# Filler products, another order of the sums of squares, a later division of x, and one 512-column product per FFN in a fourteen-stage transformer kernel

## The chip, the cores and the metric

The kernel runs on one core of one Trainium2 chip. The metric is the time of one execution in microseconds (us), as the median of a few runs. The profile was taken of one further execution.

## What is computed

Two transformer blocks follow each other on x of 256 tokens by 1024 features, in float32. The first has two layers of FFN, mixer, cross attention to a memory, FFN, with one norm ahead of each part; the mixers are a banded plus stick-breaking attention ("even") and a dilated attention ("odd"). The second has two layers of FFN, mixer ("mix": differential attention and a chunked linear recurrence, gated and merged), FFN, where the output of every part is normed once more before it is added:

```python
for l in range(DEPTH):                      # second block, cut
    h = rmsnorm(x, ffn1_norm_pre[l])
    x = x + 0.5 * rmsnorm(swiglu(h, ffn1_w_gu[l], ffn1_w_down[l]), ffn1_norm_post[l])
    h = rmsnorm(x, mix_norm_pre[l])
    ...                                     # attention, recurrence, gates -> merged
    x = x + rmsnorm(merged @ w_out[l], mix_norm_post[l])
    h = rmsnorm(x, ffn2_norm_pre[l])
    x = x + 0.5 * rmsnorm(swiglu(h, ffn2_w_gu[l], ffn2_w_down[l]), ffn2_norm_post[l])
```

## The kernel before

**Data.** x lies transposed in SBUF: 8 chunks c of 128 features by 256 tokens. Every weight matrix comes as one stream of 829 tiles of 128 by 1024 float32 (512 KB). SyncE loads tile n into one of 4 buffers `raw` once `lo_split` says that tile n-4 has been split. ScalarE rounds it to `w_hi` (L1053), VectorE makes the rest, `w_lo` = raw - w_hi (L1487); both have 6 slots. The activations are held as such a pair too (`a_hi`, `a_lo`, side by side in one tensor). A tile is multiplied chunk by chunk with three matmuls of 256 columns: w_hi by hi, w_hi by lo, w_lo by hi, so 24 matmuls to a tile, all recorded under L461 (`mm`).

**Stages.** ffn0, even, xa0, ffn1, ffn2, odd, xa1, ffn3, ffn4, mix0, ffn5, ffn6, mix1, ffn7. An FFN has 66 tiles: gate and up for each of 22 blocks j, and a down tile two blocks later. Tiles 0, 1 and 2 (gate 0, up 0, gate 1) are multiplied side by side, chunk by chunk, as the chunks of the normed x arrive (`first_three`); tile 3 (up 1) follows, then gate 2, up 2, down 0, gate 3, up 3 (tile 8), down 1, and then a loop. All engines have their own instruction list in a fixed order with semaphores between them.

**A norm.** ScalarE squares the 8 chunks into `sq` (L1084), they are added up over chunks, and a float32 product with a matrix of ones on TensorE adds over partitions; each such product shows as two records. ScalarE takes the root (L1068), VectorE the reciprocal (L1506), by which the first outputs are multiplied (L1634 and so on). After ffn4 to ffn7 the output has a norm of its own: VectorE adds the squares of chunks 0 to 5 (`part_of_squares`, L1547), and `sum_of_parts` multiplies that sum and then the squares of chunks 6 and 7. After a mix stage `sum_chunk` multiplies the squares of every chunk by itself, one behind each output tile.

**x times the root.** To avoid a reciprocal there, `post_norm` (L1598, L1602) keeps x multiplied by the root `rt`. Later x has to be divided by it: `inverse_scale` (L1553) takes the reciprocal into `rstd_m`, and `restore_x` (L1558) multiplies the 8 chunks. In an FFN both run on VectorE between the low parts of block 1 and the loop; in a mix stage `restore_x` runs between the last output tile's split and `post_norm`.

The line numbers below are those of the profile.

Of the kernel before, what the change touches and what calls it, by code (L numbers as in the profile page):

```python
# [29 lines left out]
P = 128  # L30
D = 1024
T = 256
C = D // P
# [5 lines left out]
RAW = 4  # L39
RING = 6  # L40
# [101 lines left out]
def build(nc, stream_d, x_d, mem_d, vec_d, con_d, biasa_d, biasc_d, heads_d, out_d, stages=STAGES):  # L142
    total = sum(TILES[s] for s, _ in stages)
    with ExitStack() as ctx:
# [50 lines left out]
        STAT = 6  # L195
# [5 lines left out]
        def gate_up_of(j, after_mixer):  # L201

            return bank[4 + 2 * (j % 2)][:, 0:T], bank[2 if j == 0 and after_mixer else 5 + 2 * (j % 2)][:, 0:T]
# [240 lines left out]
        def _(pe):  # L444
# [10 lines left out]
            att = [None]  # L455
            act_of = {"a": (a_hi, a_lo), "b": (b_hi, b_lo)}
            fresh = {}
            rescaled = [False]

            def mm(out, lhsT, rhs, start, stop, shared=False):  # L460
                return nc.tensor.matmul(out, lhsT, rhs, start=start, stop=stop, skip_group_check=shared)  # L461
# [81 lines left out]
            def sum_squares(stat=STAT):  # L543
# [17 lines left out]
                t.next(sq_made, C)  # L561

            def sum_of_parts():

                base = t.so_far(sq_made)
                t.next(sq_made, C)
                pe.wait_ge(root_ready, t.next(root_ready) - 1)
                pe.wait_ge(sq_second, t.next(sq_second))
                mm(bank[STAT][:, 0:T], ones, sq[:, 0, :], True, False)
                for c in (C - 2, C - 1):  # L570
                    pe.wait_ge(sq_made, base + c + 1)
                    last = mm(bank[STAT][:, 0:T], ones, sq[:, c, :], False, c == C - 1)
                last.then_inc(ss_ready, 1)

# [25 lines left out]
            def ffn(k, after_mixer):  # L600
# [4 lines left out]
                def first_three():  # L605
# [4 lines left out]
                    for c in range(C):  # L610
                        ready(c)
                        for i in range(3):
# [5 lines left out]
                            if c == C - 1:  # L618
                                last.then_inc(tile_mm, 1)

                def gate_up(n, slot, j, J):
                    for part, freed in ((0, gate_read), (1, up_read)):
                        pe.wait_ge(freed, J - 1)
                        w_tile(n + part, (slot + part) % RING, gate_up_of(j, False)[part], hi, lo)

# [14 lines left out]

                (hi, lo), h = act_of["a"], act_of["b"]
                s0 = n0 % RING
# [17 lines left out]
                at[0] += FFN_TILES  # L660
                if k >= 4:
                    sum_of_parts()
                t.next(x_ready, C)

# [303 lines left out]
            def mixer(kind, layer):  # L968
# [14 lines left out]
                if kind == "xa":  # L983
                    act_of["a"], act_of["b"] = act_of["b"], act_of["a"]
                if kind == "even":
                    stick()
# [23 lines left out]
                for k in range(C):  # L1010
                    w_next("b", y_ready)
                    if k:
                        sum_chunk(k - 1)
                sum_chunk(C - 1)
                t.next(x_ready, C)

            previous = "ffn"
            for stage, index in stages:
# [451 lines left out]
        def _(dve):  # L1470
# [143 lines left out]
            def ffn(k, following, after_mixer):  # L1614
# [58 lines left out]
                h_low(1, base + 1)  # L1673
                if rescaled[0]:
                    inverse_scale()
                    restore_x()
                first = n0 + 4 + AHEAD
                rounds = (FJ - 2) // 4
                if n0 + FFN_TILES == total:
                    rounds -= 1  # L1680
                with dve.Fori(0, rounds) as i:
                    for u in range(4):
                        def splits(e, u=u):
                            m = first + 3 * u + e
                            split(i * 12 + m, m % RAW, m % RING)
                        step(u % 2, i * 12 + (n0 + 4 + 3 * u), i * 4 + (base + 2 + u), splits)
                done[0] = first + 12 * rounds
# [311 lines left out]
            def mixer(kind, layer, following):  # L1999
# [59 lines left out]
                for k in range(C):  # L2059
                    next_tile()  # L2060
                    turn[0] += 1
                restore_x()
                dve.wait_ge(y_ready, t.next(y_ready, C))
# [290 lines left out]
```

## Time and profile before

| | us |
|---|---|
| median of 3 runs | 2635.38 (2631.01 to 2637.68) |
| the profiled execution, its own time | 2623.86 |
| its span, first to last instruction | 2622.1 |
| TensorE matmuls busy | 2545.0 (97%) |
| VectorE busy | 1802.4 (69%) |
| ScalarE busy | 1396.5 (53%) |
| mean granted TensorE clock | 0.991 |

The stages lie on the span like this, by the kernel's order and the trace: ffn4 ends at about 1400, mix0 runs to 1716, ffn5 to 1911.5, ffn6 to 2102, mix1 to 2419, ffn7 to the end. "Busy" of TensorE counts a stretch in which matmuls follow each other without a gap as full, whatever their distance from start to start; the number of matmuls in a stretch tells the distance. The profiled execution was 11.5 us shorter than the median of the runs.

### The profile page before, as it was taken

The numbers are of one execution on the slowest core, as the hardware profiler recorded it, in microseconds if no ns is written. First come the engines' busy times: TensorE is split into PE (matmuls) and PEld (weight loads), VectorE is DVE, ScalarE is ACT, GpSimd is POOL, SyncE is SP. The second block draws the span as 40 slices with busy tenths as digits, with TensorE's granted clock in tenths as the row PEclk, the third lists the DMA queues.
The fourth block names the chain that finished last, engine by engine and source line by source line (L and its number), as shares of the span: only waits on it lengthen the run. The fifth ranks groups of instructions, "written<-read, shape, count | busy, mean of one in ns | idle before, by whom it ended". The sixth has DMA issues, their size and how long they took to land.

```text
span 2622.1 us, 56431 instructions
## 1 busy us (share of the span) xinstructions
PE 2545.0 (97%) x21370; PEld 2468.5 (94%) x21370; DVE 1802.4 (69%) x2868; ACT 1396.5 (53%) x2232; POOL 190.6 (7%) x265
## 2 busy tenths in 40 slices
PE   8999799999999999999999999999999989999998
PEld 8998699999998899999998998989989989989998
DVE  6667686667667585767667657786686676676865
ACT  5456556445445655545445555654454465555543
POOL 0001001000000201000000250000000005300000
PEclk9999899999999999999999999999999999999999
DMA  7664244765564344655654543545545545335553
GB/s 270 208 192 137 81 145 157 234 211 188 195 194 155 105 164 142 201 193 180 203 193 147 182 146 113 169 161 185 184 161 192 193 147 174 129 115 176 175 193 113
DMA packets 122826, 445.89 MB, mean 170 GB/s; under 512 B 13688, under 2 KB 14712, under 8 KB 122688
## 3 DMA queue, kind: packets, MB, share of 16 engines
q1 hardware_dynamic: 120816, 436.79, 50.8%
q0 software_dynamic: 1872, 7.17, 0.8%
q8 instruction: 98, 1.61, 0.3%
q14 instruction: 40, 0.33, 0.0%
HBM read 442.86 MB, written 1.05 MB: 169 GB/s over the span
## 4 chain that ended last, share of the span: by engine, by line
PE 92%; DVE 5%; ACT 2%; issue 1%; DMA 0%; SPq 0%; DVEq 0%; ACTq 0%
PE bank L461 91%; DVE w_lo L1487 1%; PE bank L823 1%; DVE x L1558 1%; ACT w_hi L1053 1%; DVE z L1598 0%; DVE rstd_x L1506 0%; DVE x L1602 0%; DVE rstd_m L1553 0%; DVE score L1547 0%; DVE a L1514 0%; DMA raw<-in_stream_dram 0%; ACT score L1285 0%; DVE score L1538 0%; DVE z L1902 0%
## 5 line engine op out<-in xcount | busy, mean ns | idle before, releaser
L461 PE MATMUL bank<-a,w_hi 128*128 128x256 f32 x7472 | 1311.2, 280 | 37.6 <-DVE a L1514 28.0
L461 PEld LDWEIGHTS bank<-a,w_hi 128*128 128x128 f32 x7472 | 1137.1, 189 | 52.1 <-issue 47.4
L1487 DVE TENSOR_TENSOR w_lo<-raw,w_hi 128x1024 fp32r<-128x1024 f32 x829 | 1012.6, 1225 | 212.4 <-ACT w_hi L1053 210.8
L461 PE MATMUL bank<-a,w_lo 128*128 128x256 f32 x3736 | 1039.0, 278 | 0.0
L1053 ACT CAST w_hi<-raw 128x1024 fp32r<-128x1024 f32 x829 | 842.3, 1045 | 57.3 <-DMA raw<-in_stream_dram 53.8
L461 PE MATMUL bank<-b,w_hi 128*128 128x256 f32 x4800 | 839.3, 278 | 1.0 <-DVE b L1487 1.0
L461 PEld LDWEIGHTS bank<-b,w_hi 128*128 128x128 f32 x4800 | 726.8, 188 | 8.5 <-issue 3.6
L461 PEld LDWEIGHTS bank<-a,w_lo 128*128 128x128 f32 x3736 | 707.7, 189 | 0.0
L461 PE MATMUL bank<-b,w_lo 128*128 128x256 f32 x2400 | 664.9, 277 | 0.0
L461 PEld LDWEIGHTS bank<-b,w_lo 128*128 128x128 f32 x2400 | 451.4, 188 | 0.0
L1113 ACT CAST b<-hmid 128x256 fp32r<-128x256 f32 x132 | 53.8, 407 | 401.0 <-PE bank L461 389.7
L1625 DVE TENSOR_TENSOR hmid<-bank,rstd_x 128x256 f32<-128x256 f32 x168 | 71.2, 424 | 163.6 <-PE bank L461 163.5
L1109 ACT ACTIVATE sil<-sil 128x256 f32<-128x256 f32 x176 | 73.6, 418 | 145.7 <-DVE sil L1620 145.7
L1487 DVE TENSOR_TENSOR b<-hmid,b 128x256 fp32r<-128x256 f32 x132 | 56.0, 425 | 128.3 <-ACT b L1113 128.3
L461 PE MATMUL bank<-w_hi,a 128*128 128x256 f32 x736 | 130.7, 281 | 0.0
L2163 POOL TENSOR_SCALAR score<-score,rr 128x128 f32<-128x128 f32 (+1 forms) x96 | 44.5, 479 | 1114.7 <-DVE rr L1842 817.5
L461 PEld LDWEIGHTS bank<-w_hi,a 128*128 128x128 f32 x736 | 111.9, 188 | 3.4 <-issue 2.5
L1716 DVE TENSOR_TENSOR z<-bank,rstd_x 128x256 f32<-128x256 f32 x125 | 52.8, 422 | 79.0 <-PE bank L461 78.4
L461 PE MATMUL bank<-w_lo,a 128*128 128x256 f32 x368 | 102.2, 278 | 0.0
L1113 ACT CAST a<-hmid 128x256 fp32r<-128x256 f32 x44 | 17.9, 407 | 136.1 <-PE bank L461 132.5
L1639 DVE TENSOR_TENSOR hmid<-sil,hmid 128x256 f32<-128x256 f32 x176 | 74.8, 425 | 5.7
L1620 DVE TENSOR_TENSOR sil<-bank,rstd_x 128x256 f32<-128x256 f32 x160 | 67.8, 424 | 12.7 <-PE bank L461 2.8
(193 smaller groups left out, 1897.1 us busy)
## 6 DMA issues: line engine op xcount, KB each, us to landing
raw<-in_stream_dram SPq DMA_DIRECT2D x829, 512.0 KB, 3.7
z<-in_biasc_dram POOLq DMA_DIRECT2D x6, 512.0 KB, 4.9
z<-in_biasa_dram POOLq DMA_DIRECT2D x3, 512.0 KB, 4.7
x<-in_x_dram SPq DMA_DIRECT2D x2, 512.0 KB, 8.0
v<-in_mem_dram POOLq DMA_DIRECT2D x2, 512.0 KB, 5.9
out_dram<-x SPq DMA_DIRECT2D x8, 128.0 KB, 1.8
con<-in_con_dram POOLq DMA_DIRECT2D x1, 912.0 KB, 6.6
vec<-in_vec_dram POOLq DMA_DIRECT2D x1, 417.0 KB, 5.6
```

Source lines behind the costliest of these rows:

```text
L461: return nc.tensor.matmul(out, lhsT, rhs, start=start, stop=stop, skip_group_check=shared)
L823: last = nc.tensor.transpose(out[:, col:col + P], p[:, src:src + P], ident)
L1053: nc.scalar.copy(w_hi[:, slot, :], raw[:, raw_slot, :]).then_inc(hi_split, 1)
L1109: nc.scalar.activation(sil[:, jj, :], sil[:, jj, :], ACT.Silu).then_inc(silu_done, 1)
L1113: nc.scalar.copy(high_of["b"][:, jj, :], hmid[:, jj, :]).then_inc(hhi_done, 1)
L1487: return nc.vector.tensor_tensor(out, a, hi.bitcast(F32), ALU.subtract)
L1558: ins = nc.vector.tensor_tensor(x[:, c, :], x[:, c, :], rstd["m"][:, :], ALU.mult)
L1620: nc.vector.tensor_tensor(sil[:, j % 2, :], gate_up_of(j, after_mixer)[0], r, ALU.mult)\
L1625: nc.vector.tensor_tensor(hmid[:, j % 2, :], gate_up_of(j, after_mixer)[1], r, ALU.mult)\
L1639: nc.vector.tensor_tensor(hmid[:, jj, :], sil[:, jj, :], hmid[:, jj, :], ALU.mult)\
L1716: nc.vector.tensor_tensor(z[:, tile, :], out[:, 0:T], rstd[norm][:, :], ALU.mult).then_inc(w_evac, 1)
L2163: last = nc.gpsimd.tensor_scalar(p, p, rr[:, k, b:b + 1], 1.0, ALU.mult, ALU.mult)
```

## The change

- `keep_going(n)` issues n float32 products of the ones matrix with 256 columns of constants into a bank that nobody reads at that time: 1 ahead of and 7 behind `sum_of_parts` (none behind the last), 1 ahead of and 6 behind the last `sum_chunk` of a mix stage. At the kernel's start 20 products of 256 columns run on the first rounded weight tile as soon as it is there.
- `sum_of_parts` multiplies chunks 6 and 7 first and VectorE's sum last.
- In an FFN the VectorE loop is cut in two, 2 rounds and the rest, and `inverse_scale` and `restore_x` run between the two. A round is 12 tiles. In a mix stage `restore_x` runs behind the second of the last eight tiles.
- In every FFN one product of 512 columns (both halves of chunk 0, with the weights of tile 4) runs between tile 3 and tile 4, into bank 0, which the first down tile overwrites.

```diff
+            def keep_going(n):
+                for _ in range(n):
+                    mm(bank[T_BANK][:, 0:T], ones, con[:, 0:T], True, True)
 def sum_of_parts():
...
-                pe.wait_ge(sq_second, t.next(sq_second))
-                mm(bank[STAT][:, 0:T], ones, sq[:, 0, :], True, False)
                 for c in (C - 2, C - 1):
                     pe.wait_ge(sq_made, base + c + 1)
-                    last = mm(bank[STAT][:, 0:T], ones, sq[:, c, :], False, c == C - 1)
-                last.then_inc(ss_ready, 1)
+                    mm(bank[STAT][:, 0:T], ones, sq[:, c, :], c == C - 2, False)
+                pe.wait_ge(sq_second, t.next(sq_second))
+                mm(bank[STAT][:, 0:T], ones, sq[:, 0, :], False, True).then_inc(ss_ready, 1)
...
+                def wide_product(slot):
+                    mm(bank[0][:, :], w_hi[:, slot, 0:P], both[:, 0, :, :].rearrange("p a t -> p (a t)"), True, True)
...
                     for part, freed in ((0, gate_read), (1, up_read)):
                         pe.wait_ge(freed, J - 1)
+                        if j == 2 and part == 0:
+                            wait_split(n)
+                            wide_product(slot)
...
                 if k >= 4:
+                    keep_going(1)
                     sum_of_parts()
+                    keep_going(7 if k < 7 else 0)
...
+                keep_going(1)
                 sum_chunk(C - 1)
+                keep_going(6)
...
+            pe.wait_ge(hi_split, 1)
+            for _ in range(20):
+                mm(bank[T_BANK][:, 0:T], w_hi[:, 0, 0:P], w_hi[:, 0, 0:T], True, True)
...
-                if rescaled[0]:
-                    inverse_scale()
-                    restore_x()
...
-                with dve.Fori(0, rounds) as i:
...
+                for done_rounds, more in ((0, 2), (2, rounds - 2)):
+                    if done_rounds and rescaled[0]:
+                        inverse_scale()
+                        restore_x()
+                    with dve.Fori(0, more) as i:
...
                 for k in range(C):
                     next_tile()
                     turn[0] += 1
-                restore_x()
+                    if k == 1:
+                        restore_x()
```

## Rows read from the trace of the kernel before

**Rows 1.** The page: busy time by engine, and the chain's shares.

```profile
PE 2545.0 (97%) x21370; PEld 2468.5 (94%) x21370; DVE 1802.4 (69%) x2868; ACT 1396.5 (53%) x2232; POOL 190.6 (7%) x265
...
PE 92%; DVE 5%; ACT 2%; issue 1%; DMA 0%; SPq 0%; DVEq 0%; ACTq 0%
```

**Rows 2.** Windows: PE, PEld, DVE, ACT, POOL busy (x count), clock, DMA share, GB/s.

```profile
11.13:14.48 3.35, 3.35 (x16) 3.35 (x17) 2.62 (x7) 3.35 (x11) 2.24 (x4) 1.00 1.03 421
...
1404.00:1407.00 3.00, 0.46 (x4) 0.49 (x5) 2.96 (x8) 2.05 (x5) 0.00 (x0) 1.00 0.00 0
1407.10:1410.50 3.40, 3.40 (x19) 3.40 (x18) 3.40 (x11) 2.45 (x6) 0.00 (x0) 0.50 0.00 0
...
1721.10:1724.50 3.40, 3.24 (x15) 3.27 (x16) 3.40 (x11) 2.46 (x7) 0.00 (x0) 0.51 0.00 0
...
2127.30:2130.70 3.40, 3.40 (x19) 3.40 (x18) 3.40 (x5) 0.61 (x1) 0.00 (x0) 0.50 0.67 219
```

**Rows 3.** Timeline of the end of ffn4: start us, duration us, instruction [idle before it].

```profile
1399.97 1.80 DVE L1547 TENSOR_TENSOR score<-score 128x256 f32<-128x256 f32 x4
...
1401.92 1.53 PE L461 MATMUL bank<-score,con 128*128 128x256 f32 x6 [1.41 <-DVE score L1547]
1403.49 0.47 ACT L1068 ACTIVATE rt<-bank,eps 128x256 f32<-128x256 f32 x1 [2.29 <-PE bank L461]
```

**Rows 4.** Timeline of the end of mix0.

```profile
1708.41 1.23 DVE L1487 TENSOR_TENSOR w_lo<-raw,w_hi 128x1024 fp32r<-128x1024 f32 x1 [1.95 <-ACT w_hi L1053]
...
1715.91 2.77 DVE L1558 TENSOR_TENSOR x<-x,rstd_m 128x256 f32<-128x256 f32 x8
...
1716.76 0.30 PEld L461 LDWEIGHTS bank<-score,con 128*128 128x128 f32 x2 [0.44 <-ACT score L1084]
1717.49 0.48 ACT L1068 ACTIVATE rt<-bank,eps 128x256 f32<-128x256 f32 x1 [0.53 <-PE bank L461]
...
1718.71 0.42 DVE L1598 TENSOR_TENSOR z<-x,rt 128x256 f32<-128x256 f32 x1
```

**Rows 5.** Timeline of the beginning of ffn5.

```profile
1733.56 1.75 DVE L1506 RECIPROCAL rstd_x<-rstd_x 128x256 f32<-128x256 f32 x1 [0.43 <-ACT rstd_x L1068]
...
1737.39 0.47 PE L461 MATMUL bank<-a,w_hi 128*128 128x256 f32 x2 [0.27 <-DVE w_lo L1487]
...
1741.44 1.75 DVE L1553 RECIPROCAL rstd_m<-rt 128x256 f32<-128x256 f32 x1
...
1747.60 0.47 PE L461 MATMUL bank<-a,w_hi 128*128 128x256 f32 x2 [1.49 <-DVE w_lo L1487]
```

**Rows 6.** Timeline of the beginning of ffn6.

```profile
1930.02 1.75 DVE L1506 RECIPROCAL rstd_x<-rstd_x 128x256 f32<-128x256 f32 x1 [0.57 <-ACT rstd_x L1068]
...
1944.06 0.47 PE L461 MATMUL bank<-a,w_hi 128*128 128x256 f32 x2 [1.80 <-DVE w_lo L1487]
```

**Rows 7.** Timeline inside ffn5's loop: one step of VectorE and ScalarE.

```profile
1770.97 2.00 ACT L1053 CAST w_hi<-raw 128x1024 fp32r<-128x1024 f32 x2
1772.05 1.23 DVE L1487 TENSOR_TENSOR w_lo<-raw,w_hi 128x1024 fp32r<-128x1024 f32 x1 [0.70 <-ACT w_hi L1053]
```

**Rows 8.** Windows: matmuls in long even stretches of ffn1 (two), ffn5 and ffn6.

```profile
420.00:440.00 20.00, 20.00 (x172) 20.00 (x171) 17.28 (x29) 15.52 (x27) 3.08 (x3) 1.00 0.69 211
460.00:600.00 140.00, 140.00 (x1238) 140.00 (x1237) 90.61 (x122) 64.99 (x89) 2.65 (x5) 1.00 0.66 218
...
1750.00:1900.00 150.00, 150.00 (x1276) 150.00 (x1275) 95.34 (x129) 68.84 (x93) 0.00 (x0) 1.00 0.60 197
...
1950.00:2090.00 140.00, 140.00 (x1237) 140.00 (x1237) 90.88 (x125) 65.36 (x89) 0.00 (x0) 1.00 0.62 203
```

**Rows 9.** Timeline of the kernel's start.

```profile
4.17 1.04 ACT L1053 CAST w_hi<-raw 128x1024 fp32r<-128x1024 f32 x1 [2.14 <-DMA raw<-in_stream_dram]
...
11.13 0.77 PE L461 MATMUL bank<-a,w_hi 128*128 128x256 f32 x2 [11.13 <-DVE a L1514]
...
22.02 0.48 ACT L1068 ACTIVATE rstd_x<-bank,eps 128x256 f32<-128x256 f32 x1 [2.81 <-PE bank L461]
```

More of the change, by code:

```diff
@@ L456, in _ @@
             act_of = {"a": (a_hi, a_lo), "b": (b_hi, b_lo)}
+            two_of = {"a": a_two, "b": b_two}
             fresh = {}
@@ L639, in down @@
                     last.then_inc(tile_mm, 1)
-                (hi, lo), h = act_of["a"], act_of["b"]
+                (hi, lo), h, both = act_of["a"], act_of["b"], two_of["a"]
                 s0 = n0 % RING
@@ L984, in mixer @@
                     act_of["a"], act_of["b"] = act_of["b"], act_of["a"]
+                    two_of["a"], two_of["b"] = two_of["b"], two_of["a"]
                 if kind == "even":
@@ L1680, in ffn, with splits @@
                     rounds -= 1
-                with dve.Fori(0, rounds) as i:
[L1682 to L1686, printed above, removed]
+                for done_rounds, more in ((0, 2), (2, rounds - 2)):
[3 more added lines that the diff above has]
+                    with dve.Fori(0, more) as i:
+                        for u in range(4):
+                            def splits(e, u=u):
+                                m = first + 12 * done_rounds + 3 * u + e
+                                split(i * 12 + m, m % RAW, m % RING)
+                            step(u % 2, i * 12 + (n0 + 4 + 12 * done_rounds + 3 * u),
+                                 i * 4 + (base + 2 + 4 * done_rounds + u), splits)
                 done[0] = first + 12 * rounds
```

## Prediction

> **What bounds the kernel now.** I read the page first: TensorE's matmuls fill 97% of the span and 92% of the chain that ended last [rows 1]. So nothing that VectorE, ScalarE or the DMA do matters except where TensorE waits for it, and the questions are where TensorE stands still, where its clock is low, and how far apart its matmuls start while it is "busy". The chain in order of time showed where other engines enter it: stick-breaking in the even mixer, which the change does not touch, and the seams ffn4-mix0, mix0-ffn5, ffn5-ffn6, ffn6-mix1, mix1-ffn7 and the end.
>
> At the seams I read windows and the timeline. Behind ffn4 TensorE waits 1.41 us for VectorE's sum, runs the three sum products in 1.53 us [rows 3] and then waits about 3 us for root, product and low part of chunk 0: 0.46 us busy in the next 3 [rows 2]. Behind this gap the granted clock is 0.50 for 3.4 us: 19 matmuls in 3.40 us at 1.2 GHz against some 30 at 2.4 [rows 2]. The same stands at mix0-ffn5 [rows 2], ffn5-ffn6 and mix1-ffn7. In mix1 the low stretch comes 20 us later, behind other waits [rows 2].
>
> In the heads of ffn5, 6 and 7 TensorE later waits twice for `w_lo`: 0.27 us at tile 5, and 1.49, 1.80 and 1.49 us at tile 8, because VectorE takes the reciprocal and divides x there (1.75 us, then 8 multiplications in 2.8 us) [rows 5, 6].
>
> Last, the spacing. At full clock, 1238 matmuls fill 140 us of ffn1: 113.1 ns from start to start. The same instructions in ffn5 need 150 us for 1276: 117.6 ns [rows 8]. ffn1 itself runs 172 in 20 us (116 ns) before its sum product and 113 ns after it. So there are two paces at one clock, about 4.5 ns apart; a pace, once taken, stays until TensorE waits or runs a float32 product, and it is taken anew at each restart. In this trace ffn5 kept the slow one from tile 8 to its end: 58 tiles x 24 x 4.5 ns = 6.3 us.
>
> **The change, part by part.**
>
> *Order of the sums (ffn4 to ffn7).* Three products take 1.53 us, 0.45 from start to start and 0.17 of modelled end [rows 3]. Two of them leave the path behind VectorE's sum: 0.9 us each time. In front of them now stand a filler (0.45) and the two others, whose last square ends some 0.4 us before VectorE's sum; that queue delays the last product by 0 to 0.25. I take 0.8 x 4 = 3.2 us. In the mix heads everything that follows hangs on VectorE's chain (products, fold of the squares, low parts, two reciprocals), so there this is the only gain, whatever the clock.
>
> *Last sum of a mix stage.* The root is ready at 1717.97, VectorE starts its products at 1718.71 because the division of x ran until then [rows 4]. Moved behind the second output tile the division is free: VectorE idles about 1.95 us per tile there [rows 4]. That is 0.74 saved. The filler ahead of the last sum product has only 0.44 us of gap [rows 4] behind the product before it and lasts 0.45, with its weight loads: I charge 0.3. Net 0.44 x 2 = 0.9 us.
>
> *Fillers behind the sums.* 7 x 0.45 = 3.2 us stand between the last sum product and the first low part about 3.1 us later; 6 x 0.45 = 2.7 in a gap of 3.6. Free, if the first products of the norm are not ready sooner. They do no work; their worth is the clock. If it stays at 2.4 GHz, the 19 matmuls of 3.40 us take about 2.15 (19 x 0.113). The 1.25 to 1.5 us are not all path: chunks arrive every 1.13 us and need 9 x 0.113 = 1.02, so TensorE then follows VectorE. What shows is the wait that disappears: the reciprocal's idle of 0.43, 0.57 and 0.43 us for the root, which waits for TensorE's sum in tile 3 [rows 5, 6]. 1.4 us together; lower bound 0, if the clock falls all the same; upper 1.5 x 3, if VectorE's order did not bind.
>
> *Later division in the FFN.* The waits at tile 8 go: 1.49 + 1.80 + 1.49, and 0.17 each by which the last matmul's modelled end hides idle time: 5.3 us. The work (4.5 us) goes into the loop. There VectorE finishes the low half of a tile at 1773.28, and that tile is four behind the one that TensorE has just begun at 1770.5 [rows 7]: used at about 1781.7, 8 us later. 4.5 fit in, and VectorE idles over 2 us per step, so the lead is back after two steps. If it did not fit, TensorE would stop once per FFN, up to the whole 4.5. Next late is tile 5, whose wait grows to about 1 us since TensorE arrives earlier; this is in the sum, since all is counted from VectorE's chain. Cutting the loop in two adds a loop end, under the same cover.
>
> *Wide product.* No row shows 512 columns; two of 256 take 0.227 us [rows 8], which I take as price; 0 where a wait follows. In ffn5 to 7 tile 5's wait swallows it, in ffn0 to 4 nothing does: 5 x 0.22 = 1.1 us lost. Bank 0 is free then.
>
> *Start.* The first rounded tile is there at 5.2 us, the first real product at 11.13 [rows 9], and 16 matmuls run in 3.35 us until 14.48 before the pace doubles [rows 2]: at most 1.5 us to win. 20 products at the low clock (0.213 each) fill 5.3 to 9.6. Whether the clock is up at 11.13, after 1.5 us or more of idling, is open: between 0 and 1.5, and VectorE's three copies allow only 0.9 of it up to the reciprocal. I take 0.8. On this the Trainium skill (TensorE: Matmul & The Clock Gate, Part 1) says that the monitor's window runs freely and does not begin with the kernel, so that the number of slow matmuls differs from run to run; by it this term is anything from 0 to 1.5 in any one run. The trace cannot contradict it with one start.
>
> *mix1's low stretch* at 2127 [rows 2] may stay, vanish or get a twin in mix0, since TensorE idles there a little more: 0, plus or minus 1.7.
>
> **The sum:** 3.2 + 0.9 + 1.4 + 5.3 + 0.8 - 1.1 = 10.5 us. From 2623.86 of the profiled execution: 2613.4. The runs shown have a median 11.5 us higher, at 2635.38; I take the gain as the same there and predict 2624.9.
>
> **Rivals.**
>
> *Pace for the better.* The 11.5 us between median and profiled execution are close to two further FFNs at the slow pace (2 x 6.3): the timed runs may well have ffn5, 6 and 7 all slow. If fewer restarts and the wide product leave one or two more FFNs at the fast pace, 6 to 13 us come on top: 2612 to 2619. For: float32 products between others did end the slow pace in ffn1 [rows 8]. Against: tile 5's wait comes behind the wide product, and the pace is taken anew after it; the restart at tile 8 led to the slow pace in ffn5 and to the fast one in ffn6 [rows 8]. The Trainium skill (same page, Part 2 on issue gaps and LDWEIGHTS) has loads pulled ahead of running matmuls and prices 128 weight columns at 107 ns, 256 moving columns at 109; by that one long product gives the loads a lead, and this rival would hold. Its 109 ns agree with neither pace here (113.1 and 117.6); the measurements decide.
>
> *No use of fillers or order (same).* The clock falls in spite of fillers, the start wins nothing, and the queue eats the reordering: 5.3 + 1.5 + 1 of the sums - 1.1 = 6.7 us or less: 2629. For: the clock also fell at 2127, where no long gap of TensorE lies ahead [rows 2]. Against: with the fillers TensorE is busy nearly throughout.
>
> *Pace for the worse (slower).* If the wide product turned the pace slow in ffn0 to ffn4, where it is fast now and no wait follows that would change it, each would lose 62 x 24 x 4.5 ns = 6.7 us, five 33: 2658. From two FFNs on it outweighs the whole gain. For: nobody has seen what it does; a pace is sticky. Against: the float32 products, as long, led to the fast one.
>
> **Numbers.** The sum as it stands 0.5 (2618 to 2630, since terms and one pace may go either way), pace for the better 0.22, no use 0.18, pace for the worse 0.1. A measurement can tell 0.3%, 7.9 us: faster means below 2627.5. Of the first case four fifths lie there, of the second all, of the third a fifth; faster 0.66, same 0.24, slower 0.10. The range 2611 to 2634 holds the first three but for their edges.
>
> **What the profile after would show.** Clock 1.00 at all five seams; three sum products with VectorE's last; PE's waits for `w_lo` in ffn5 to 7 once, about 1 us at tile 5, none at tile 8; L1553 and L1558 in the loop's middle with no wait of PE near them; matmul counts per 140 us of every FFN. The prediction is wrong if those counts change (1238 or 1190), if PE waits in the middle of an FFN, or if the fillers still run when the first low part is ready.

## The result and the profile after

The changed kernel takes 2654.26 us (median of 8 runs, 2645.55 to 2661.74), the kernel before 2634.34 us beside it (8 runs, 2626.21 to 2642.14): a ratio of 1.0082, 95% interval 1.0060 to 1.0104. It is 0.8% slower. The forecast was 2624.9 with a range of 2611 to 2634, so the result lies on the other side and far outside. The profiled execution took 2658.42 us (span 2656.6), 34.6 us more than the profiled execution of before.

The page of after, busy time by engine and the chain's shares:

```profile
PE 2608.1 (98%) x21476; PEld 2529.5 (95%) x21476; DVE 1803.0 (68%) x2868; ACT 1396.9 (53%) x2232; POOL 190.5 (7%) x265
...
PE 93%; DVE 4%; ACT 2%; issue 0%; DMA 0%; SPq 0%; DVEq 0%; ACTq 0%
```

Against [rows 1], TensorE is busy for 63.1 us more with 106 more records; VectorE has 0.6 us more. The 106 records are the 39 float32 products of two records each, the 20 at the start and the 8 wide ones; at 0.43, 0.213 and 0.23 us a product that is some 23 us. For the other 40 the same matmuls take longer, or stand further apart. Windows inside the FFNs of after (columns as in [rows 2]) show it:

```profile
460.00:600.00 140.00, 140.00 (x1191) 140.00 (x1190) 89.62 (x122) 63.02 (x86) 2.64 (x5) 1.00 0.65 215
650.00:790.00 140.00, 140.00 (x1191) 140.00 (x1190) 87.75 (x120) 62.79 (x86) 0.00 (x0) 1.00 0.60 196
...
1265.00:1405.00 140.00, 140.00 (x1191) 140.00 (x1190) 88.33 (x121) 62.86 (x86) 0.00 (x0) 1.00 0.60 195
1780.00:1920.00 140.00, 140.00 (x1238) 140.00 (x1237) 95.10 (x133) 65.64 (x89) 0.00 (x0) 1.00 0.61 201
1970.00:2110.00 140.00, 140.00 (x1191) 140.00 (x1190) 90.72 (x126) 61.90 (x86) 0.00 (x0) 1.00 0.59 192
```

The clock reads 1.00 in all of them, and 1191 matmuls are through where [rows 8] had 1238 in ffn1. All five of ffn0 to ffn4 read 1191, ffn6 and ffn7 too; ffn5, the slow one of before, is now the fast one. Where does ffn0 change? The timeline of TensorE around its wide product:

```profile
24.18 0.28 PE L462 MATMUL bank<-a,w_lo 128*128 128x256 f32 x1
24.29 0.39 PE L462 MATMUL bank<-a,w_hi 128*128 128x256 f32 x2
24.52 0.28 PE L462 MATMUL bank<-a,w_lo 128*128 128x256 f32 x1
24.63 0.62 PE L462 MATMUL bank<-a,w_hi 128*128 128x512 f32 x3
25.09 0.28 PE L462 MATMUL bank<-a,w_lo 128*128 128x256 f32 x1
...
25.44 0.28 PE L462 MATMUL bank<-a,w_lo 128*128 128x256 f32 x1
...
25.80 0.28 PE L462 MATMUL bank<-a,w_lo 128*128 128x256 f32 x1
```

A group of three matmuls (one of `w_lo`, two of `w_hi`) starts 0.34 us after the one ahead of it before the product, and 0.35 to 0.36 us after it behind the product (the timeline rounds to 0.01). From one `w_lo` to the next across the product it is 0.57 us: 0.23 more than a group, so the product itself costs what two of 256 columns would, as forecast. What follows it is what costs.

The end of ffn4 and the beginning of ffn5 in after, timelines:

```profile
1434.95 0.60 PE L462 MATMUL bank<-con 128*128 128x256 f32 x2
1435.68 1.53 PE L462 MATMUL bank<-score,con 128*128 128x256 f32 x6
1437.05 3.19 PE L462 MATMUL bank<-con 128*128 128x256 f32 x14
1437.25 0.47 ACT L1088 ACTIVATE rt<-bank,eps 128x256 f32<-128x256 f32 x1 [1.44 <-PE bank L462]
...
1752.93 0.47 ACT L1088 ACTIVATE rt<-bank,eps 128x256 f32<-128x256 f32 x1 [0.65 <-PE bank L462]
1753.51 0.42 DVE L1618 TENSOR_TENSOR z<-x,rt 128x256 f32<-128x256 f32 x1 [2.20 <-ACT rt L1088]
1756.06 0.47 PE L462 MATMUL bank<-a,w_hi 128*128 128x256 f32 x2 [0.58 <-DVE a L1534]
...
1767.84 1.75 DVE L1526 RECIPROCAL rstd_x<-rstd_x 128x256 f32<-128x256 f32 x1
...
1771.66 0.47 PE L462 MATMUL bank<-a,w_hi 128*128 128x256 f32 x2 [0.38 <-DVE w_lo L1507]
...
1835.29 1.75 DVE L1573 RECIPROCAL rstd_m<-rt 128x256 f32<-128x256 f32 x1
1837.07 2.77 DVE L1578 TENSOR_TENSOR x<-x,rstd_m 128x256 f32<-128x256 f32 x8
1840.07 1.23 DVE L1507 TENSOR_TENSOR w_lo<-raw,w_hi 128x1024 fp32r<-128x1024 f32 x1 [0.23 <-DVE x L1578]
```

ScalarE idles 1.44 us ahead of its root behind ffn4, where [rows 3] had 2.29: 0.85 won. VectorE starts its products 0.58 us after the root's start at the end of mix0, where [rows 4] had 1.22: 0.64 won. The reciprocal of ffn5's head has no idle time before it any more ([rows 5]: 0.43). The only wait for `w_lo` in this head is 0.38 us, at tile 5. The division runs at 1835, in mid-FFN, with no wait of TensorE beside it. So the named gains are there, and over them lies a loss of another kind.

### The profile page after: what moved, and what is told of

Its sections match the earlier page's. It is cut to its first block, busy times and chain, and to the rows that moved or that the text cites. A ratio compares the mean times of both kernels' runs of the same rounds, so it can differ in the third digit from the quotient of the medians.

```text
span 2656.6 us, 56661 instructions
## 1 busy us (share of the span) xinstructions
PE 2608.1 (98%) x21476; PEld 2529.5 (95%) x21476; DVE 1803.0 (68%) x2868; ACT 1396.9 (53%) x2232; POOL 190.5 (7%) x265
## 4 chain that ended last, share of the span: by engine, by line
PE 93%; DVE 4%; ACT 2%; issue 0%; DMA 0%; SPq 0%; DVEq 0%; ACTq 0%
PE bank L462 92%; PE bank L837 1%; DVE x L1622 1%; DVE z L1618 1%; DVE w_lo L1507 0%; DVE a L1534 0%; DVE score L1558 0%; DVE rstd_x L1526 0%; DMA x<-in_x_dram 0%; ACT score L1305 0%; ACT w_hi L1073 0%; ACT a L1094 0%; DVE z L1924 0%; DVE z L1927 0%; DVE z L1930 0%
## 5 line engine op out<-in xcount | busy, mean ns | idle before, releaser
L462 PE MATMUL bank<-a,w_hi 128*128 128x256 f32 x7478 | 1333.0, 282 | 9.0 <-DVE w_lo L1507 6.4
L462 PE MATMUL bank<-b,w_hi 128*128 128x256 f32 x4802 | 857.2, 281 | 1.0 <-DVE b L1507 1.0
L462 PEld LDWEIGHTS bank<-b,w_hi 128*128 128x128 f32 x4802 | 737.3, 189 | 8.4 <-issue 3.6
```

## The experiments

All compare with the kernel before, run on the same chip beside them. Where a kernel adds products, their outputs are overwritten or read by nothing, and no part of the computation is left out; kernels that take fillers away leave out only such products. In the diffs `wide_product(slot, n)` multiplies `n` columns of both activation blocks into bank 0, and `float_product(out)` multiplies the constant ones with 256 float32 columns (0.45 us).

The kernel before has medians of 2627.31 to 2631.46 us in these comparisons and 2634.34 in the first, so two kernels that were not compared side by side are best compared by their ratios.

Since several kernels are compared by place, here is the difference to the profiled execution of before in each stage, in us. It is taken at the moment when VectorE ends the low part of the same stream tile, up to the end of the span.

| stage | after | e1, no wide | e5, float32 at tile 7 | e7, e5 without fillers |
|---|---|---|---|---|
| start to tile 6 | +0.1 | -1.3 | -1.1 | +1.4 |
| rest of ffn0, mixer | +7.3 | -1.7 | 0.0 | -2.2 |
| ffn1 to ffn4, mixer between | +26.0 | +0.3 | -1.1 | +0.7 |
| end of ffn4 | +0.4 (+0.9 of pace, -0.4 behind it) | -0.9 | -0.9 | -0.9 |
| mix0 | +1.6 | +5.0 | +3.3 | 0.0 |
| head of ffn5 | -3.7 | -2.8 | -3.1 | -2.3 |
| rest of ffn5 | -5.1 | 0.0 | -5.1 | -5.1 |
| head of ffn6 | -2.4 | -3.4 | -3.1 | -1.4 |
| rest of ffn6, mix1 | +7.6 | -0.9 | +0.8 | -1.7 |
| head of ffn7 | -2.2 | -3.1 | -2.4 | -2.2 |
| rest | +5.1 | -0.6 | -0.6 | -0.6 |
| sum | +34.6 | -9.1 | -13.3 | -14.2 |

**e1_after_no_wide**: the changed kernel without its wide product.

```diff
-                        if j == 2 and part == 0:
-                            wait_split(n)
-                            wide_product(slot)
```

> The changed kernel without its 512-column product, all else kept. Theory (the 512-column product turns TensorE's pace from 113 to 117.6 ns per matmul, and nothing turns it back until the FFN ends): ffn0 to ffn4 are back at about 1238 matmuls per 140 us, 5 x 6.7 = 33 us shorter than the changed kernel, so about 2620 us, and 10 us under the kernel before; ffn5 to 7 may lie at either pace. Rival (the fillers at the start and the seams, or the cut loop of VectorE, set the slow pace): ffn0 to ffn4 stay at 1191 per 140 us and the time at about 2654.

Measured: 2614.29 us (6 runs, 2604.97 to 2618.22) beside 2627.31, ratio 0.9947 (0.9929 to 0.9966). One of its windows, in ffn4:

```profile
1250.00:1390.00 140.00, 140.00 (x1238) 140.00 (x1237) 88.57 (x120) 62.85 (x86) 0.00 (x0) 1.00 0.60 194
```

ffn0 to ffn4 are fast again; ffn5 is slow, ffn6 and ffn7 fast, as in before. Eight products of 0.23 us, 1.8 us of work, are worth some 35 us by the ratios (1.0082 against 0.9947) and 40 by the medians.

**e2_only_wide**: the kernel before with only the wide product, at the same place.

```diff
+                        if j == 2 and part == 0:
+                            wait_split(n)
+                            wide_product(slot)
```

> The kernel before with nothing but the 512-column product between tiles 3 and 4 of each FFN. Theory: ffn0 to ffn4 at 1191 per 140 us, 33 us and 1 us of products over the kernel before, about 2668 us. Rival (the product only does harm together with fillers or the cut loop): at most 2 us over the kernel before, 1238 per 140 us.

Measured: 2672.69 us (4 runs, 2651.90 to 2676.18), ratio 1.0149 (1.0103 to 1.0195). All eight FFNs are at the slow pace in its profile, of 2676.18 us:

```profile
460.00:600.00 140.00, 140.00 (x1191) 140.00 (x1190) 88.04 (x120) 62.96 (x86) 2.65 (x5) 1.00 0.65 215
```

By these two the wide product alone sets the loss, with or without the other edits.

**e3_mixed**: before, with a different insert in each of ffn0 to ffn4 ahead of tile 4, and a float32 product in ffn5 to ffn7 at tile 8, behind its wait.

```diff
+                        if j == 2 and part == 0:
+                            wait_split(n)
+                            if k == 0:
+                                wide_product(slot, 256)
+                            if k in (1, 2, 4):
+                                wide_product(slot)
+                            if k == 1:
+                                wide_product(slot)
+                            if k == 2:
+                                float_product(bank[0][:, 0:T])
+                        if k >= 5 and j == 3 and part == 1:
+                            wait_split(n + 1)
+                            float_product(gate_up_of(j, False)[part])
```

> The kernel before with another insert in each FFN in place of the 512-column product, so that one trace shows which of them turns the pace. ffn0: one float32r product of 256 columns; ffn1: two of 512; ffn2: one of 512 and behind it a float32 product of 256; ffn3: nothing; ffn4: one of 512; ffn5 to 7: nothing before tile 4, but a float32 product of 256 columns at tile 8, behind its wait for w_lo. If length against the weight load matters: ffn0 and ffn3 1238 per 140 us, ffn1 and ffn4 1191, ffn2 1238 since the float32 product sets the fast pace, and ffn5 to 7 all 1238. If a 512-column product toggles the pace: ffn1 is fast. If float32 products do not set the pace (rival: coincidence in the trace before), ffn2 stays slow and ffn5 to 7 are mixed.

Measured: 2643.47 us (one execution). Its windows in ffn1 (two wide products) and ffn4 (one):

```profile
460.00:600.00 140.00, 140.00 (x1238) 140.00 (x1237) 90.01 (x123) 64.87 (x88) 2.63 (x5) 1.00 0.66 219
...
1250.00:1390.00 140.00, 140.00 (x1191) 140.00 (x1191) 85.61 (x116) 61.03 (x83) 0.00 (x0) 1.00 0.57 190
```

ffn0 (one of 256 columns), ffn1 (two wide), ffn2 (wide, then float32) and ffn3 (nothing) are fast, ffn4 (one wide) is slow. In ffn1 the second wide product takes back what the first did. Behind tile 8's wait a float32 product set nothing: ffn5 and ffn6 came out slow, ffn7 fast.

**e4_float_behind_wait**: after without the wide product, with one float32 product in a running stream in ffn5 and ffn7 and behind tile 5's wait in ffn6.

```diff
+                        if k in (5, 7) and j == 3 and part == 0:
+                            wait_split(n)
+                            float_product(gate_up_of(j, False)[part])
+                        if k == 6 and j == 2 and part == 1:
+                            wait_split(n + 1)
+                            float_product(gate_up_of(j, False)[part])
```

> The changed kernel without its 512-column product, with one float32 product of ones by constants (256 columns, 0.45 us) in ffn5 and ffn7 ahead of tile 7 and in ffn6 at tile 5 behind its wait. Theory: all eight FFNs at the fast pace, 1238 per 140 us; about 6.7 us less for each of ffn5 to 7 that is slow in the run without it, so 2610 to 2614 us, and a smaller spread from run to run. Rival (the pace behind a restart is not to be set): mixed paces in ffn5 to 7 and the time of the run without the product.

Measured: 2612.36 us (4 runs, 2611.14 to 2614.62), ratio 0.9947 (0.9927 to 0.9967). ffn5 and ffn7 are fast and ffn6 is slow (1191 in 140 us). Only ffn5 speaks for the product in the stream: 5.4 us ahead of it hold 47 matmuls there, but 49 in ffn7, as many as behind it, so ffn7 was fast already. In ffn6 the stream was slow ahead of the wait, and the product behind the wait left it so.

**e5_float_tile7**: after without the wide product, and a float32 product ahead of tile 7 in ffn5, ffn6 and ffn7, behind their last wait.

```diff
+                        if k >= 5 and j == 3 and part == 0:
+                            wait_split(n)
+                            float_product(gate_up_of(j, False)[part])
```

> The changed kernel without the 512-column product and with one float32 product ahead of tile 7 in ffn5, ffn6 and ffn7, where TensorE does not wait. Theory (a float32 product amid running matmuls sets the fast pace, one behind a wait does not): all eight FFNs at 1238 per 140 us, 6 us under the run that had the product of ffn6 behind a wait, about 2606 us. Rival (ffn5 and ffn7 were fast by chance in that run): one or two of the three are slow, 2612 to 2618 us.

Measured: 2610.68 us (6 runs, 2607.37 to 2613.32) beside 2630.29, ratio 0.9916 (0.9892 to 0.9941): the lowest median of all, though the intervals of e1, e4, e6 and e7 overlap with it. Windows ahead of the product in ffn5, behind it, and over ffn5:

```profile
1736.70:1742.20 5.50, 5.50 (x48) 5.50 (x48) 5.49 (x10) 4.08 (x6) 0.00 (x0) 1.00 0.67 203
...
1743.00:1748.50 5.50, 5.50 (x50) 5.50 (x50) 4.54 (x8) 3.40 (x6) 0.00 (x0) 1.00 0.91 316
...
1755.00:1895.00 140.00, 140.00 (x1238) 140.00 (x1237) 92.53 (x129) 63.53 (x86) 0.00 (x0) 1.00 0.57 194
```

48 against 50 in equal stretches (each count includes the matmuls cut by the edges): slow, then fast. The same in ffn6 and ffn7. So all eight are fast, and e5 is 5.1 us better than e1 just in "rest of ffn5".

**e6_no_start** and **e7_no_fillers**: e5 without the 20 products at the start; and without any filler.

```diff
-            for _ in range(20):
-                mm(bank[T_BANK][:, 0:T], w_hi[:, 0, 0:P], w_hi[:, 0, 0:T], True, True)
...
-                    keep_going(1)
                     sum_of_parts()
-                    keep_going(7 if k < 7 else 0)
...
-                keep_going(1)
                 sum_chunk(C - 1)
-                keep_going(6)
```

> The same without the 20 products at the start. Theory (they raise the clock for the first products in some runs only): 0 to 1.3 us slower in the median; in the profile the first 3.4 us behind the first real product at half clock. Rival (they change the pace of ffn0): ffn0 at 1191 per 140 us.

> The same without any filler product, at the start or at the seams. Theory (the seam fillers hold the clock at ffn5, ffn6 and ffn7, which shows as the wait of the reciprocal for the root, 1.4 us in all, while the order of sums and the division keep their gains): 1.4 to 3 us slower than with all fillers, the clock 0.50 behind each seam again. Rival (the fillers carry most of the gain): 6 us or more slower.

Measured: e6 2612.41 us (5 runs, 2609.29 to 2612.97), ratio 0.9917 (0.9889 to 0.9945); e7 2611.43 us (7 runs, 2609.61 to 2618.41), ratio 0.9933 (0.9911 to 0.9955). All three intervals overlap; no filler is worth anything that can be measured here. Where the clock was low, first in e5, then in e7:

```profile
1423.40:1426.80 3.40, 3.40 (x18) 3.40 (x18) 3.25 (x7) 1.05 (x1) 0.00 (x0) 0.51 0.80 276
...
2116.30:2119.70 3.40, 3.40 (x19) 3.40 (x18) 3.40 (x7) 1.05 (x1) 0.00 (x0) 0.51 0.92 294
```

```profile
1405.70:1409.10 3.40, 3.40 (x17) 3.40 (x17) 3.40 (x11) 2.48 (x7) 0.00 (x0) 0.50 0.00 0
...
1423.00:1426.40 3.40, 2.22 (x19) 2.25 (x20) 3.40 (x5) 0.04 (x1) 0.00 (x0) 1.00 0.36 125
```

e5 has its low stretches inside the mix stages, four of them, and none at a seam; e7 has them at the seams and none inside. In the table the fillers win 0.8, 1.7 and 0.2 us in the three heads (e5 against e7) and lose 3.3 in mix0 and 2.5 in "rest of ffn6, mix1". The other traces bear this out, with numbers that change from one to the next: with the seam fillers mix0 holds no low stretch in e10, one in after, e4 and e9, and two in e1, e5, e6 and e11, and costs 0.7, 1.4 to 1.6 and 3.2 to 5.0 us more than in before. In those seven a low stretch begins some 21 to 23 us behind the root of ffn4's end, and in none of the six without fillers. So in mix0 the low stretch was mostly moved, not saved.

**e8_toggles**: before, with other inserts, at tile 4 and, in ffn1 and ffn3, once more ahead of tile 7.

```diff
+                            if k in (0, 1, 3):
+                                wide_product(slot)
+                            if k == 0:
+                                wide_product(slot)
+                                wide_product(slot)
+                            if k == 2:
+                                wide_product(slot, 384)
+                            if k == 4:
+                                wide_product(slot, 128)
+                        if j == 3 and part == 0 and k in (1, 3):
+                            wait_split(n)
+                            if k == 1:
+                                mm(bank[6][:, :], w_hi[:, slot, 0:P], both[:, 0, :, :].rearrange("p a t -> p (a t)"), True, True)
+                            else:
+                                float_product(bank[6][:, 0:T])
```

> The kernel before with another insert ahead of tile 4 in each FFN. ffn0: three products of 512 columns; ffn1: one of 512, and one of 512 ahead of tile 7; ffn2: one of 384; ffn3: one of 512, and a float32 product ahead of tile 7; ffn4: one of 128. Theory (each 512-column product turns the pace over, a float32 product within a stream sets the fast one): ffn0 slow (1191 per 140 us), ffn1 fast from tile 7 on (1238), ffn3 fast from tile 7 on. ffn2 and ffn4 tell which lengths turn it; if an odd number of half products does, both are slow. Rival (one 512-column product sets the slow pace and the fast ffn1 of the mixed run was chance): ffn1 slow.

Measured: 2660.64 us (one execution). Its windows: ffn0; ffn1 between its two wide products and behind them; ffn3; ffn4:

```profile
30.00:170.00 140.00, 140.00 (x1191) 140.00 (x1190) 87.98 (x120) 62.47 (x86) 2.11 (x4) 1.00 0.61 210
455.90:464.30 8.40, 8.40 (x72) 8.36 (x72) 8.40 (x15) 6.56 (x11) 0.00 (x0) 1.00 0.52 172
470.00:610.00 140.00, 140.00 (x1238) 140.00 (x1237) 89.54 (x123) 63.27 (x86) 2.63 (x5) 1.00 0.63 215
...
1080.00:1220.00 140.00, 140.00 (x1191) 140.00 (x1190) 86.10 (x117) 60.42 (x82) 0.00 (x0) 1.00 0.55 187
1270.00:1410.00 140.00, 140.00 (x1191) 140.00 (x1191) 85.60 (x117) 60.60 (x83) 0.00 (x0) 1.00 0.55 186
```

Three wide products leave ffn0 slow, as one does. In ffn1 the first slows the stream and the second, three tiles later, makes it fast. 128 columns act like 512 (ffn4), 384 like 256 (ffn2 fast, 1238). And the float32 product of ffn3, in a running stream, did not cure what a wide product had done: it is no sure remedy. The traces hold many more such cases, since each FFN has sum products of its own. In ffn5 to ffn7 it is one, in the middle of tile 3; with the inserted ones at tile 7, one float32 product in a running stream met a slow pace 28 times in the fourteen traces, and the pace was fast behind it 17 times and slow 11 times. A fast pace it left fast, 27 times of 27. In ffn0 to ffn4 two such products stand in a row ahead of tile 3, and wherever they ran without a wait in front the pace was fast behind them: 53 times from slow, as in ffn1 of before [rows 8], and 12 times from fast. That is how ffn0 to ffn4 come to be fast in before. Two in a row at tile 7, as a remedy, were not tried.

**e9_two_wide**: after, with the wide product twice.

```diff
                             wide_product(slot)
+                            wide_product(slot)
```

> The changed kernel with a second 512-column product right behind the first in every FFN: more work, nothing taken away. Theory (each such product turns the pace over, two leave it as it was): ffn0 to ffn4 at 1238 per 140 us, about 33 us under the changed kernel and 1 to 2 us over it without any such product, about 2616 us. Rival (any 512-column product sets the slow pace, or costs time by itself): 2655 us or more.

Measured: 2619.47 us (10 runs, 2612.61 to 2629.85) beside 2631.46, ratio 0.9958 (0.9932 to 0.9984). ffn0 to ffn4 read 1237 or 1238:

```profile
460.00:600.00 140.00, 140.00 (x1237) 140.00 (x1237) 90.69 (x124) 64.27 (x88) 2.64 (x5) 1.00 0.66 220
```

Eight more products, and the kernel is some 33 us faster than after by the ratios, 35 by the medians. It is the plainest test of the theory: no cost that grows with the products, by their duration, banks or operands, can be the cause, since all are doubled.

ffn5 to ffn7 are fast too, and two of them show what a pure toggle can't explain. In ffn5 the pace was slow ahead of the two products, 0.35 to 0.36 us from one `w_lo` to the next, and fast behind them, 0.34:

```profile
1738.78 0.28 PE L462 MATMUL bank<-a,w_lo 128*128 128x256 f32 x1
...
1739.14 0.28 PE L462 MATMUL bank<-a,w_lo 128*128 128x256 f32 x1
...
1742.03 0.28 PE L462 MATMUL bank<-a,w_lo 128*128 128x256 f32 x1
...
1742.37 0.28 PE L462 MATMUL bank<-a,w_lo 128*128 128x256 f32 x1
```

ffn6 went the same way. So two wide products led to the fast pace from either one; they don't simply leave it as it was.

**e10_old_division**: e5 with the division of x back in the FFN's head.

```diff
+                if rescaled[0]:
+                    inverse_scale()
+                    restore_x()
...
-                    if done_rounds and rescaled[0]:
-                        inverse_scale()
-                        restore_x()
```

> The changed kernel without the 512-column product, with the float32 product ahead of tile 7, and with the division of x in the FFNs back at its old place (in the mix stages it stays at the new one). Theory: waits of 1.5 to 2 us for w_lo at tile 8 of ffn5, 6 and 7 come back, 5 us in all, and with them a new draw of the pace behind tile 8, up to 6.3 us for each FFN that draws the slow one: 2616 to 2630 us and a wide spread. Rival (the later division gains nothing, since VectorE only idles elsewhere): 2611 us.

Measured: 2625.02 us (10 runs, 2613.03 to 2631.28), ratio 0.9981 (0.9953 to 1.0009): 14 us above e5 by the medians, about 17 by the ratios. TensorE waits 11.1 us for `w_lo` in the whole profile, ten times, against 7.2 and seven times in e5: 3.9 us. The rest is the pace. The wait at tile 8 lies behind the float32 product and drew anew; ffn5 and ffn7 came out slow:

```profile
2465.00:2605.00 140.00, 140.00 (x1191) 140.00 (x1190) 86.08 (x116) 60.62 (x82) 0.00 (x0) 1.00 0.54 179
```

ffn0 was slow too in this execution (1192), with nothing changed there. It was slow from its first tiles on, ahead of the sum products: 62 matmuls in the 7 us from 12 on, first here, then in e5, 64:

```profile
12.00:19.00 7.00, 7.00 (x62) 7.00 (x61) 4.58 (x11) 6.89 (x16) 3.79 (x6) 1.00 0.92 365
```

```profile
12.00:19.00 7.00, 7.00 (x64) 7.00 (x64) 4.53 (x9) 6.85 (x15) 3.31 (x6) 1.00 0.88 357
```

**e11_old_order**: e5 with the sum products in their old order, VectorE's first.

```diff
+                pe.wait_ge(sq_second, t.next(sq_second))
+                mm(bank[STAT][:, 0:T], ones, sq[:, 0, :], True, False)
                 for c in (C - 2, C - 1):
                     pe.wait_ge(sq_made, base + c + 1)
-                    mm(bank[STAT][:, 0:T], ones, sq[:, c, :], c == C - 2, False)
-                pe.wait_ge(sq_second, t.next(sq_second))
-                mm(bank[STAT][:, 0:T], ones, sq[:, 0, :], False, True).then_inc(ss_ready, 1)
+                    last = mm(bank[STAT][:, 0:T], ones, sq[:, c, :], False, c == C - 1)
+                last.then_inc(ss_ready, 1)
```

> The same as the last but with the new division, and with the old order of the three sum products at the end of ffn4 to ffn7. Theory: 0.8 us each, 3.2 us slower than with the new order, about 2614 us. Rival (with the filler in front the order is worth nothing): 2611 us.

Measured: 2615.85 us (10 runs, 2609.33 to 2617.56), ratio 0.9943 (0.9919 to 0.9966). Its interval overlaps that of e5, so by the time this is open; the sign and size (about 5 us) don't contradict 3.2. The profiled execution had ffn0 slow as well, so it can't be compared with e5's as a whole. But the term can be read off at its place. ScalarE's wait ahead of the root at ffn4's end, in e11 and then in e5:

```profile
1407.36 0.47 ACT L1093 ACTIVATE rt<-bank,eps 128x256 f32<-128x256 f32 x1 [2.28 <-PE bank L462]
```

```profile
1400.40 0.47 ACT L1092 ACTIVATE rt<-bank,eps 128x256 f32<-128x256 f32 x1 [1.44 <-PE bank L462]
```

At the ends of ffn4 to ffn7 it is 2.28, 2.28, 2.29 and 1.99 us with the old order and 1.44 each time with the new: 3.1 us together, with the filler in front in both.

**e12_before_again**: the kernel before, unchanged, profiled a second time.

> The kernel before, profiled once more. Theory (its runs spread by 20 us because ffn5, 6 and 7 draw their pace anew at tile 8): another set of slow FFNs than ffn5 alone, ffn0 to ffn4 fast again, and the time of the run off 2623.9 by about 6.3 us for each slow FFN more or less. Rival (the spread has another source): the same paces and another time, or the same time and other paces.

Measured: 2630.21 us, 6.35 us more than the first profile. Its windows in ffn5, ffn6 and ffn7:

```profile
1760.00:1900.00 140.00, 140.00 (x1191) 140.00 (x1191) 86.17 (x118) 61.37 (x84) 0.00 (x0) 1.00 0.58 191
1955.00:2095.00 140.00, 140.00 (x1237) 140.00 (x1237) 90.06 (x123) 64.33 (x87) 0.00 (x0) 1.00 0.61 199
2460.00:2600.00 140.00, 140.00 (x1191) 140.00 (x1190) 87.64 (x118) 62.54 (x84) 0.00 (x0) 1.00 0.56 186
```

ffn7 is slow here and was fast in the first profile. Ahead of tile 8's wait the stream of ffn7 is slow in both profiles; behind it, it is fast in the first and slow in the second. Up to the end of mix1 the two profiles are 0.4 us apart, at the last tile of ffn7 5.9 us; 6.3 were computed for one slow FFN. The same program takes one path or the other.

## Why the prediction was wrong

**The step that failed** is the one on the wide product: "two of 256 take 0.227 us, which I take as price", "5 x 0.22 = 1.1 us lost". The price of the product itself was right (0.23 us across it). But the step took the price as the whole effect, although the paragraph on spacing had shown two sticky paces, and left the effect on the pace to a rival, at a chance of 0.1. That rival, "each would lose 62x24x4.5 ns = 6.7 us, five 33: 2658", is what happened. Between their first and last tiles ffn0 to ffn4 lost 6.4 to 7.0 us each, 33 together (the table's rows have 33.3 and 0.9 at the end of ffn4, about 1 of it in the mixers between). e1 and e2 show that the product is the cause; e3, e8 and e9 that its effect is a turn of the pace and no cost in itself. The argument against that rival, "the float32 products, as long, led to the fast one", compared products by their duration, and not even that was alike: a float32 product takes 0.43 to 0.45 us, and only each of its two records, 0.22, is about as long as the wide product's 0.23. In e8 the shortest of all, 128 columns, turns the pace as 512 do, and 384 leave it.

**ffn5 to ffn7.** "In ffn5 to 7 tile 5's wait swallows it" held for the cost and not for the pace. In ffn5 of after the 24 matmuls between the product and tile 5's wait are fast where the stream ahead was slow, in ffn6 and ffn7 they are slow where it was fast, and behind the wait each stayed so to its end (-5.1, +4.7 and +5.1 us). Whether the product or the wait settled these three isn't shown, since a wait can change the pace. "The pace is taken anew after a wait" is supported by e3, e4, e10 and e12, but anew doesn't mean another: of 53 waits of over 0.1 us in the heads of ffn5 to ffn7, over all fourteen traces and without those that have an insert right behind them, 18 turned a fast pace slow, 4 a slow one fast, and 31 left it. Ffn5 of before was slow from tile 5's wait on, not only from tile 8's, as the prediction had it. One consequence of the draws was left out of the forecast: the later division, by removing tile 8's wait, also removes a draw. The 3.9 us of e10's waits and two slow FFNs at some 5 us, as in its profile, are about the 14 us it costs, where the waits alone were priced at 5.3; that its timed runs had two slow FFNs on average isn't shown.

**Order of the sums (3.2).** The root's wait behind ffn4 is 0.85 us shorter, and the stage gave 0.9 in e1, e5 and e7; 0.8 was forecast. In after only 0.4 of it is left when the next stage's first tiles are reached. The roots' waits of e11 against e5 give 3.1 us over the four ends; in time e11 can't tell it from nothing.

**Last sum and division of a mix stage; clock fillers; later division.** The heads of ffn5, ffn6 and ffn7 gained 3.7, 2.4 and 2.2 us in after and 2.8, 3.4 and 3.1 in e1, against about 2.5, 3.3 and 2.5 by the forecast's terms. The waits at tile 8 are gone in all three, as said; tile 5's is 0.4 to 0.5 us in after, where the wide product fills part of it, and 0.5 to 0.8 in e1, not 1. The division in the loop disturbed nothing.

**The fillers' worth (1.4)** is the second step that failed. They did hold the clock at all seams, and the heads gained from it (0.8 + 1.7 + 0.2 us, e5 against e7). But in e5 mix0 and mix1 hold two low stretches each, 3.4 us at half speed, where before had one in mix1 [rows 2] (and one in mix0 as well in e12) and e7 none, and they gave back more. The prediction had this as "plus or minus 1.7", centred on nothing; it should have been charged in both mixes. Since e7 can't be told from e5 in time, the value for the sum is 0 as far as is shown. The windows of after in the two mix heads:

```profile
1458.70:1462.10 3.40, 3.16 (x15) 3.19 (x16) 3.40 (x7) 0.00 (x0) 0.00 (x0) 0.51 0.59 171
...
2155.00:2158.40 3.40, 3.29 (x15) 3.32 (x16) 3.40 (x6) 0.21 (x1) 0.00 (x0) 0.50 0.60 172
```

**The start (0.8).** 0 in after, 1.3 in e1 and 1.1 in e5, but 1.5 lost in e9; e6 and e7, without it, lost 1.0 and 1.4 against before. In after 17 matmuls ran in 3.72 us at the low pace from 10.98 on, as in [rows 2]. The executions differ with nothing changed ahead of this point. With this agrees what the Trainium skill (TensorE: Matmul & The Clock Gate, Part 1) says, that the monitor runs freely and doesn't start with the kernel. The ratios of e5 and e6 are equal, so even its mean worth isn't shown.

**The mean of the runs.** The prediction read the 11.5 us between the profiled execution and the median as further slow FFNs. e12 supports it: one more cost 6.35 us, and with 6.3 us for each of three FFNs of before the times would spread over 19 us; 25 runs of before spread from 2617.66 to 2645.47, 28 us, so something else varies too; a slow ffn0, as e10 and e11 had it, would be one candidate, which no profile of before shows.

Without the wide product the sum would have been 11.6 us. e1 gave 9.1 by the spans of the profiled executions and 13.0 by the medians (2627.31 less 2614.29). So the mechanism of the other parts, the fillers apart, was right, and the total about right; 5.0 us were given back in mix0.

## What to carry to other kernels

When a stream of equal matmuls fills nearly the whole time, look at the spacing of its starts, not only at busy time: 4% at full clock is invisible in the page's busy shares, and with all eight FFNs slow in its profile e2's median lay 45 us above the kernel before. An insertion into such a stream isn't priced by its duration; count the matmuls of an equal window ahead of it and behind it, and try it with the insertion doubled, which here turned a loss of 0.8% into a gain of 0.4%. And filling an engine's gap for the sake of the clock can move the low stretch to the next gap, as it did here; whether filling that one too would pay wasn't tried. What helped was fewer waits (the later division) together with a float32 product behind the last of them, since a wait could draw the pace anew.

## What the runs showed of the hardware that was not expected

Matmuls of 256 float32r columns with a weight load for each run at two paces under a granted clock of 1.00: 1238 or 1191 in 140 us, 113.1 and 117.6 ns. (The counts take in matmuls that the edges cut; from start to start in the trace it is 113.3 and 117.8 ns.) The pace stays to the end of an FFN, for some 60 tiles of 24 matmuls.

What turned it in a running stream:

| product | pace behind it | cases |
|---|---|---|
| one of 512 columns | the other one, 20 of 20 | fast to slow: ffn0 to ffn4, ffn6 and ffn7 of after, all of e2, ffn4 of e3, ffn1 and ffn3 of e8; slow to fast: ffn5 of after, the second one in ffn1 of e8 |
| two of 512 | fast, 9 of 9 | from fast: ffn1 of e3, ffn0 to ffn4 and ffn7 of e9; from slow: ffn5 and ffn6 of e9 |
| three of 512 | fast to slow | ffn0 of e8 |
| one of 128 | fast to slow | ffn4 of e8 |
| one of 256; one of 384 | left fast | ffn0 of e3; ffn2 of e8 |
| one float32 | from fast: fast, 27 of 27; from slow: fast 17, slow 11 | the sum products in tile 3 of ffn5 to ffn7; tile 7 of e4 to e7, e10, e11 and ffn3 of e8 |
| two float32 in a row | fast, 53 from slow and 12 from fast | the sum products ahead of tile 3 in ffn0 to ffn4 |

The cases aren't independent, since many are the same place of the program in several traces. Where TensorE waited ahead of the two sum products (ffn0 of e1, e4, e5, e10 and e11), they left the pace as it was, slow in e10 and e11.

A wait of TensorE can draw the pace anew: the unchanged ffn7 of before was fast in one execution and slow in the other. Ffn0 was also slow in two (e10, e11) of six profiled executions with the start products and no single wide product behind them (the others: e1, e4, e5, e9), and in none of five without start products (before, e3, e6, e7, e12): too few to blame the start. In e6, without them, the first tiles were slow as well, and the sum products made them fast.

What stays open is which state is kept. A phase with two positions would explain ffn1 of e3 and ffn0 to ffn4 of e9, where two equal products cancel, but not ffn5 and ffn6 of e9, where they turned slow to fast. The lengths fit no simple count of columns (128 and 512 turn it over, 256 and 384 leave it, one case each but for 512), and one float32 product does both. The one sign in the records is its own spacing: its two records start 217 to 218 ns apart in the 11 cases that left a slow pace slow, and 215 to 216 in the 17 that ended it. What holds such a phase wasn't settled.
